# Attention steps in another order: scores, values, weight unit, transposes, in a two-block float32 transformer kernel

## The reference, cut to what matters

```
h = rmsnorm(x, norm_mix[l])
qa, ka, va, qb_, kb, vb, qc, kc, vc, gate_logits = split(h @ w_in[l])
# mixer a: 8 heads of 64, 2 key heads, queries and keys normed and rotated
q = axial_rope(rmsnorm(q, qg), rope);  k = axial_rope(rmsnorm(k, kg), rope)
p = softmax(q k / 8);                  y_a = p v
# mixer b: 8 heads, a window of 128, a bias, and a sink in the softmax
m = maximum(max(sc, axis=-1), sk);     e = exp(sc - m)
p = e / (sum(e, axis=-1) + exp(sk - m))
# mixer c: 4 heads, two maps each, subtracted
lam = exp(sum(lq1 * lk1)) - exp(sum(lq2 * lk2)) + lambda_init
p = softmax(sc + bias);                attn = p[:, :, :, 0] - lam * p[:, :, :, 1]
o = rmsnorm(attn v, subln_g) * (1 - lambda_init)
# merge
merged = sum(sigmoid(gate_logits) * (ys @ w_branch), branches)
x = x + merged @ w_out[l]
```

## Time and profile before

| what | us |
| --- | --- |
| median of 3 runs | 2630.56 (2629.4 to 2631.21) |
| the profiled execution: its own time | 2628.28 |
| the profiled execution: its span | 2626.5 |
| PE busy | 2574.3 (98% of the span) |
| DVE busy | 1559.0 (59%) |
| ACT busy | 1370.0 (52%) |
| POOL busy | 271.3 (10%) |

### The profile page before, as it was taken

One profiled execution on the slowest core, in us unless ns is written; L12 is line 12 of the kernel. 1 busy time (PEld: TensorE's weight loads), 2 busy tenths in 40 slices (PEclk: granted clock), 3 DMA queues, 4 the chain that ended last, 5 costly groups with the idle time before them and its releaser, 6 DMA issues.

```text
span 2626.5 us, 39446 instructions
## 1 busy us (share of the span) xinstructions
PE 2574.3 (98%) x14932; PEld 2251.6 (86%) x14932; DVE 1559.0 (59%) x2105; ACT 1370.0 (52%) x2155; POOL 271.3 (10%) x180
## 2 busy tenths in 40 slices
PE   8999999999999999999999999999999999999998
PEld 6889999888888899898888888988888888888887
DVE  5558645555555774656555556667555555677654
ACT  5547445544544663655445444655445445465543
POOL 0200210000000002100100001552000000344000
PEclk9999999999999999999999999999999999999999
DMA  6555314455555541347655554235555555334553
GB/s 246 191 179 172 103 62 146 143 185 186 203 188 184 169 145 57 105 150 211 197 184 188 188 174 164 97 113 185 184 192 183 186 188 165 121 106 159 189 188 138
DMA packets 118205, 427.55 MB, mean 163 GB/s; under 512 B 13020, under 2 KB 14812, under 8 KB 117660
## 3 DMA queue, kind: packets, MB, share of 16 engines
q1 hardware_dynamic: 117552, 424.59, 48.4%
q10 hardware_dynamic: 492, 0.69, 0.1%
HBM read 423.79 MB, written 1.44 MB: 162 GB/s over the span
## 4 chain that ended last, share of the span: by engine, by line
PE 89%; DVE 6%; ACT 3%; issue 1%; DMA 1%; DVEq 0%; POOL 0%; ACTq 0%; SPq 0%
PE bank L480 73%; PE bank L987 2%; DVE lo_slots L468 2%; PE bank L676 1%; PE bank L1655 1%; PE bank L500 1%; ACT hi_slots L454 1%; PE bank L1694 1%; PE bank L1671 1%; PE bank L622 1%; PE bank L1147 1%; PE bank L1158 1%; PE bank L1156 1%; PE bank L1840 1%; PE bank L1816 1%
## 5 line engine op out<-in xcount | busy, mean ns | idle before, releaser
L468 DVE TENSOR_TENSOR lo_slots<-raw,hi_slots 128x1024 fp32r<-128x1024 f32 x732 | 900.7, 1235 | 736.9 <-ACT hi_slots L454 736.6
L454 ACT ACTIVATE hi_slots<-raw 128x1024 fp32r<-128x1024 f32 x788 | 830.2, 1057 | 663.3 <-PE bank L480 653.0
L480 PE MATMUL bank<-hi_slots,x_hi_room 128*128 128x512 f32 x1536 | 609.4, 397 | 4.3 <-DVE lo_slots L445 3.8
L480 PE MATMUL bank<-hi_slots,x_lo_room 128*128 128x512 f32 x1536 | 600.3, 391 | 0.0
L480 PE MATMUL bank<-lo_slots,x_hi_room 128*128 128x512 f32 x1536 | 599.5, 390 | 0.0
L480 PEld LDWEIGHTS bank<-hi_slots,x_hi_room 128*128 128x128 f32 x1536 | 289.1, 188 | 64.0 <-DVE lo_slots L445 4.6
L480 PEld LDWEIGHTS bank<-hi_slots,x_lo_room 128*128 128x128 f32 x1536 | 288.9, 188 | 61.5
L480 PEld LDWEIGHTS bank<-lo_slots,x_hi_room 128*128 128x128 f32 x1536 | 289.4, 188 | 57.1
L480 PE MATMUL bank<-x_hi_room,hi_slots 128*128 128x256 f32 x1152 | 332.4, 289 | 3.7 <-DVE x_lo_room L652 1.8
L480 PE MATMUL bank<-x_lo_room,hi_slots 128*128 128x256 f32 x1152 | 321.6, 279 | 0.0
L480 PE MATMUL bank<-x_hi_room,lo_slots 128*128 128x256 f32 x1152 | 321.4, 279 | 0.0
(11 more groups left out here) (327 smaller groups left out, 3197.4 us busy)
## 6 DMA issues: line engine op xcount, KB each, us to landing
raw<-w_full SPq DMA_DIRECT2D x792, 512.0 KB, 3.3
bias_mem<-bias_rows SPq DMA_DIRECT2D x8, 288.0 KB, 6.7
mem<-mem_t SPq DMA_DIRECT2D x2, 1024.0 KB, 7.8
const<-consts SPq DMA_DIRECT2D x1, 1664.0 KB, 7.0
h<-x_t SPq DMA_DIRECT2D x2, 512.0 KB, 6.1
final<-finals SPq DMA_DIRECT2D x2, 512.0 KB, 6.5
out_t<-h SPq DMA_DIRECT2D x4, 256.0 KB, 2.2
bias_rows<-junk ACTq DMA_DIRECT2D x1, 384.0 KB
```

The lines of the kernel that those rows point to most:

```text
L454: nc.scalar.activation(w_hi[s], raw[s][:, :], ACT.Copy).then_inc(hi_ready[s], 1)
L468: nc.vector.tensor_tensor(w_lo[s], raw[s][:, :], w_hi[s].bitcast(F32), ALU.subtract).then_inc(lo_ready[s], 1)
L480: mm = nc.tensor.matmul(out, lhsT=a, rhs=b, start=start and n == 0, stop=stop and n == len(passes) - 1)
```

## The change

Seven edits, all in the order or the number of instructions. The same tiles, banks and matmuls remain.

1. PE runs a step as scores(i), values(i-2), unit(i), transposes(i-1): the transposes go to the end of the step.
2. ACT runs a step as output copy(i-3), gate tanh(i-1), transposed copy(i-2), high part of the next unit, exponentials(i). The transposed copy is now one step later in its numbering, since the transposes end their step.
3. DVE computes the maximum of map i ahead of the product of map i-1.
4. The negation L1791 is folded into the maximum (`negate=True`) for a and c maps and for the first block's cross attention. For b maps one operation takes the maximum with the sink and negates.
5. The sink's difference (L1794) goes: ACT's exponential takes the sink as its bias.
6. The rotation takes the keys' chunk first, and lambda's three operations stand right behind that chunk.
7. PE no longer waits for lambda ahead of the scores. DVE waits for it at the first c difference.

```
-ROPE_CHUNKS = ((0, 2), (2, 4), (4, 5))
+ROPE_CHUNKS, ROPE_DONE = ((4, 5), (0, 2), (2, 4)), (1, 3, 5)
...
+        def act_gate_out(E, g):
+            act.wait_ge(*unit_done(E, E.mid(5, g)))
+            nc.scalar.activation(sig[:, g, :], bank[2 + g % 2][:, 0:TOK], ACT.Tanh, scale=0.5).then_inc(bank_free[g % SLOTS], 1)
...
         def pe_attention(E, maps):
...
-                if 1 <= i <= len(maps) and maps[i - 1]["use"] is not None:
...            (the transposes of map i-1, between the scores and the values)
                 if i >= 2 and maps[i - 2]["use"] is not None:
...            (values)
                     pe_gate(E, g)
                 for m in branches_at(E, i):
                     pe_branch_unit(E, m)
+                if 1 <= i <= len(maps) and maps[i - 1]["use"] is not None:
...            (the same transposes, behind the unit)
         def act_attention(E, maps):
...
+                for g in gates_at(E, i - 1):
+                    act_gate_out(E, g)
+                if 2 <= i < len(maps) + 2 and maps[i - 2]["use"] is not None:
+                    u = maps[i - 2]["use"]
+                    act.wait_ge(sems["pt_ps"], E.after("pt_ps", u + 1))
+                    if u >= 2:
+                        act.wait_ge(sems["y_ps"], E.after("y_ps", u - 1))
+                    nc.scalar.activation(probs_t[:, u % 2, :], bank[6 + u % 2][:, :], ACT.Copy).then_inc(sems["pt_sb"], 1)
+                for g in gates_at(E, i - 1):
+                    split_hi(E, E.mid(5, g))
...            (the exponentials of map i follow)
-                        act.wait_ge(sems["s_sinkdiff"], E.after("s_sinkdiff", m["biased"] + 1))
-                        nc.scalar.activation(st[:, 8:10], st[:, 8:10], ACT.Exp).then_inc(sems["s_sinkexp"], 1)
+                        nc.scalar.activation(st[:, 8:10], st[:, 2:4], ACT.Exp,
+                                             bias=p2(E, "sink", m["head"])).then_inc(sems["s_sinkexp"], 1)
         def dve_attention(E, maps):
...            (the maximum of map i now stands ahead of the product of map i-1)
-                    nc.vector.tensor_reduce(st[:, 0:2], heads(scores, TT), AX_X, ALU.max).then_inc(sems["s_max"], 1)
-                    dve.wait_ge(sems["s_max"], E.after("s_max", i + 1))
...
-                    nc.vector.tensor_scalar(st[:, 2:4], st[:, 0:2], -1.0, None, ALU.mult).then_inc(sems["s_neg"], 1)
+                    if m["kind"] != "b":
+                        nc.vector.tensor_reduce(st[:, 2:4], heads(scores, TT), AX_X, ALU.max, negate=True).then_inc(sems["s_neg"], 1)
+                    else:
+                        nc.vector.tensor_reduce(st[:, 0:2], heads(scores, TT), AX_X, ALU.max).then_inc(sems["s_max"], 1)
+                        dve.wait_ge(sems["s_max"], E.after("s_max", m["biased"] + 1))
+                        nc.vector.tensor_scalar(st[:, 2:4], st[:, 0:2], p2(E, "sink", m["head"]), -1.0, ALU.max,
+                                                ALU.mult).then_inc(sems["s_neg"], 1)
...
+                        if m["head"] == HEADS:
+                            dve.wait_ge(sems["lam"], E.after("lam", 3))
...
-                        pe.wait_ge(sems["lam"], E.after("lam", 3))
```

More of the change, by code:

```diff
@@ L1701, in pe_attention @@
                     pe_branch_unit(E, m)
+                if 1 <= i <= len(maps) and maps[i - 1]["use"] is not None:
+                    m = maps[i - 1]
+                    u = m["use"]
+                    if m["kind"] == "c":
+                        pe.wait_ge(sems["s_diff"], E.after("s_diff", m["head"] - HEADS + 1))
+                    else:
+                        pe.wait_ge(sems["s_p"], E.after("s_p", 2 * i))
+                    if u >= 2:
+                        pe.wait_ge(sems["pt_sb"], E.after("pt_sb", u - 1))
+                    src = probs[:, (i - 1) % 3, :]
+                    for kt in range(TT):
+                        for t in range(TT):
+                            at = kt * TOK + t * P
+                            mm = nc.tensor.transpose(bank[6 + u % 2][:, at:at + P], src[:, t * TOK + kt * P:t * TOK + kt * P + P],
+                                                     c("ident"))
+                    mm.then_inc(sems["pt_ps"], 1)
         def act_attention(E, maps):
@@ L1705, in act_attention @@
             for i in range(len(maps) + 3):
[L1706 to L1711, removed]
                 if i >= 3 and maps[i - 3]["use"] is not None:
@@ L1748, in dve_attention @@
             for i in range(len(maps) + 4):
[L1749 to L1765, removed]
-                        nc.vector.scalar_tensor_tensor(out=probs[:, n % 3, :], in0=probs[:, n % 3, :], scalar=lam[:, 3:4],
-                                                       in1=probs[:, (n - 1) % 3, :], op0=ALU.mult,
-                                                       op1=ALU.add).then_inc(sems["s_diff"], 1)
                 if i < len(maps):
@@ new lines, in dve_attention @@
+                if 1 <= i <= len(maps):
+                    m = maps[i - 1]
+                    n = i - 1
+                    st = stat[:, n % 3, :]
+                    dve.wait_ge(sems["s_exp"], E.after("s_exp", 2 * n + 2))
+                    if m["kind"] == "b":
+                        dve.wait_ge(sems["s_sinkexp"], E.after("s_sinkexp", m["biased"] + 1))
+                        nc.vector.tensor_tensor(st[:, 4:6], st[:, 4:6], st[:, 8:10], ALU.add).then_inc(sems["s_sinksum"], 1)
+                        dve.wait_ge(sems["s_sinksum"], E.after("s_sinksum", m["biased"] + 1))
+                    nc.vector.reciprocal(st[:, 6:8], st[:, 4:6]).then_inc(sems["s_rec"], 1)
+                    dve.wait_ge(sems["s_rec"], E.after("s_rec", n + 1))
+                    for t in range(TT):
+                        nc.vector.tensor_scalar(probs[:, n % 3, tile_cut(t)], probs[:, n % 3, tile_cut(t)],
+                                                st[:, 6 + t:7 + t], None, ALU.mult).then_inc(sems["s_p"], 1)
+                    if m["kind"] == "c" and n % 2:
+                        if m["head"] == HEADS:
+                            dve.wait_ge(sems["lam"], E.after("lam", 3))
+                        dve.wait_ge(sems["s_p"], E.after("s_p", 2 * n + 2))
+                        nc.vector.scalar_tensor_tensor(out=probs[:, n % 3, :], in0=probs[:, n % 3, :], scalar=lam[:, 3:4],
+                                                       in1=probs[:, (n - 1) % 3, :], op0=ALU.mult,
+                                                       op1=ALU.add).then_inc(sems["s_diff"], 1)
@@ L1935, in dve_cross_max @@
             dve.wait_ge(sems["s_ps"], E.after("s_ps", i + 1))
-            nc.vector.tensor_reduce(st[:, 0:2], heads(bank[4 + i % 2][:, :], TT), AX_X, ALU.max).then_inc(sems["s_max"], 1)
-            dve.wait_ge(sems["s_max"], E.after("s_max", i + 1))
-            nc.vector.tensor_scalar(st[:, 2:4], st[:, 0:2], -1.0, None, ALU.mult).then_inc(sems["s_neg"], 1)
+            nc.vector.tensor_reduce(st[:, 2:4], heads(bank[4 + i % 2][:, :], TT), AX_X, ALU.max,
+                                    negate=True).then_inc(sems["s_neg"], 1)
         def dve_cross_p(E, i):
```

59 lines of the change are left out of this document (18 added, 41 removed).

## The result

| | us | ratio to the kernel before |
| --- | --- | --- |
| before, 6 runs on the same chip | 2629.66 (2625.97 to 2631.21) | |
| changed, 6 runs | 2640.4 (2638.98 to 2642.06) | 1.0043, 95% interval 1.003 to 1.0056 |
| changed, span of the profiled run | 2639.6 (before 2626.5) | |

Slower by 10.7 us, where 6.9 were forecast. The granted clock over the span is 0.998.

The account below looks back on a forecast made before the run. PE, busy 98% of the span, was taken as the bound, leaving its waits in the second block's attention. Layers of 133.0 against 129.3 and 129.7 add 7.0: 2628.28 becomes 2635.3 profiled, median 2637.5, range 2632 to 2643 us.

Parts of the forecast that it names:

- The start: Before each layer's first scores: PE's wait of about 4.3 us and the half clock go, gaining 6.9 and 7.3 us.
- a steps: Attention steps of a maps: POOL's low part holds DVE's products, so a step takes 5.26 us from scores to scores.
- the clears: POOL's clears for the keys in the attention: 0.27 us in the sum of a layer.
- b: Attention steps of b maps: the sink's maximum and then the products wait for POOL, so a step takes 5.68 us.
- A pair of c: Even plus odd attention steps of c maps: even 5.79 us behind DVE's held products, odd at PE's own 4.48 plus 0.05.
- Step 3: An attention step in which POOL is busy with the keys' clears and the product passes: 4.97 us.
- step 2: An early attention step, counted among the five a steps at 5.26 us each.
- The rotation: Rotation in another order, a shorter chunk ahead: nothing waits for it sooner, 0, not over 0.3 us either way.
- The negations: Fused negations on DVE in the attention: worth nothing on the path; the cross attention's negation also 0.
- the first: Rival for the attention steps: POOL's hold does not reach the products, gain 20.2 us, so 2610.3; chance 0.16.
- The second: Rival for the attention steps: only the a products pass, saving 2.4 us a layer, so 2632.7; chance 0.15.
- The third: Rival for the start: POOL delays the last query sum, half clock stays, costing 4.5 us a layer, 2646.5; chance 0.10.

Follow-up runs that it names:

- the short-hold run: The changed kernel with POOL's low part computed for only the first 64 of 1024 columns, so the output is not the reference's: 2613.0 us, ratio 0.9942.

## Why the prediction was right, and where it was not

The direction and the mechanism held, and 2640.4 lies inside the stated 2632 to 2643. That it does is in part luck: the rotation below, 2.8 us, was not among the errors for which that width was left. The changed kernel is slower since each step's products now come behind the maximum, where POOL's low part has started and holds them.

- **The start**: as forecast. PE goes from the third gate unit into the scores at 1633.26 without a wait and at a granted clock of 1.00. POOL ran 7.83 us for its three low parts from 1629.27, and the last query sum (2.12 instead of 0.69) ended at 1632.42, in time. The sine product before it, with an operand in PSUM, took 0.68 under the same operation.
- **a steps**: 5.26 forecast, 5.18 measured for those free of the clears. **b**: 5.68 forecast, 5.70 to 5.79. **A pair of c**: 5.79 + 4.53 = 10.32 forecast, 10.32 to 10.39. The loop of copy, high part, low part, products and transposes is right as to its members.
- **Step 3** was mis-sized: 4.97 forecast, 5.57 measured. I wrote that the product passes under the keys' clears. POOL goes from the clears through the copies into the next low part without a pause (1646.04 to 1652.37), and L1788 takes 3.16, to 0.16 behind the low part. In step 2 the first product ends behind the low part (1646.12) and the second takes 0.91 beside a clear of 0.77, and the step is 5.74 where 5.26 were forecast. Together the two steps are 11.31, where the sum had 10.50 with its 0.27 for the clears. Seven b steps are 0.4 longer than forecast and the other a steps 0.3 shorter. A layer's attention is 134.1 and 134.0 instead of 133.0: 2.1 us in all.
- **The rotation** is the term that failed: "Nothing waits for it sooner, 0, and not over 0.3 either way". By the traces it is 1.4 a layer (the three pairs of times, 0.3 to 2.9 us for both layers, have the same sign and are too coarse for the size). I asked who waits for the rotated chunk, and not what the moved reciprocal had covered: DVE's wait for ACT's high part. The profile had both durations, 3.35 and 1.75.
- **The negations** were costed at nothing. In this order they would have cost 6.6 us if left apart. The sum wasn't hurt, since it was made for the folded form, but the reason I gave for the nothing is wrong.
- **What bounds the kernel before**: I took its 9.88 and 5.11 as waits of the order. With the low parts on DVE the same order gives 8.8 to 9.4 and 4.91.

With 2.1 for the steps and 2.8 for the rotation my sum would be 2642.4. The runs gave 2640.4. Of the 2.0 between them 0.9 is the base: the sum starts from 2630.56, and the six runs of the kernel before have 2629.66. The remaining 1.1 is less than the 2.1 by which the medians of the kernel before differ between the sets (2629.7 to 2627.6).

Of the rivals, the first (the hold does not reach the products, 2610.3) is refuted by L1788's 2.76. Its time is right for a kernel in which there is no hold: the runs that took it away, or what it held, came to 2608 to 2615. The second (only the products of a pass) and the third (the start isn't gained) are refuted by the rows above.

The Trainium skill, "SBUF — State Buffer", section "SBUF: two separate sides", says that DVE in a 2-port mode, or with two SBUF inputs against a GpSimd operation that reads SBUF, shares a pair of ports with GpSimd that is locked for a whole instruction, and that the other side fully blocks. The trace agrees: with maximum and negation apart, L1772 on 128x2 stood 2.12 under an operation of 2.37. "VectorE: DVE Perf Modes", section "The perf-mode tier table", lists a float32 reduce at 1x only, with no 2-port form, and the maximum took 0.69 beside POOL in every run here.

## What to carry to other kernels

Before an operation of DVE is moved past another, lay POOL's timeline beside it: here a product, a sum or a scalar operation with its inputs in SBUF that came behind the start of POOL's low part stood until that ended, even one on two numbers per partition (2.76 for L1788, issued 0.05 behind it, and 1.75 for L1774), while the maximum (0.69) and the sine product with an operand in PSUM (0.68) passed. If POOL shares a pipeline step with DVE, try the same work on DVE before reordering anything: here DVE did it in half the time, and it was worth 10 us in the old order (2619.3 to 2609.9) and 25 in the changed kernel. And for an operation that is moved "for free", ask also which wait it was filling.

## What the runs showed that I had not expected

- PE has two paces for the same unit of 24 matmuls, at a granted clock of 1.00: 2.74 to 2.75 and 2.83. Most runs of the new order alternate between them, the short-hold run has 2.83 nearly throughout its first layer, the old order with low parts on DVE 2.75 in all its a and b steps. Two runs with the same code in the steps (the start's edits with the new and the old rotation) have a steps of 4.92 and 5.00 in the first layer, and both about 4.92 in the second. It is up to 0.08 in some 20 steps a layer, 3 us in two layers. What sets it stays open.
- In the new order the values take 0.95 and in the old 0.87, with a wait of their weight load for the copy of 0.24 on average (7.8 us in 32).
- A reciprocal on DVE takes 3.35 us for 128x512, about five times the 0.69 of a product of that size, and 1.75 for 128x256, where the product takes 0.42. On 128x2 it took 0.15 beside POOL's low part (L1785 at 1638.47, POOL from 1638.40), so it was not held.
